# Rotary positions moved into the projection stream, a later wait for the router weights, and an earlier clearing of the expert accumulator

## The reference, cut to what matters

```
h   = layer_norm(x) * (1 + scale) + shift
p   = h @ w_in                          # q, k, v of A and B, conv inputs, q, k, v, o, gates of D
yA  = windowed attention of rope(qA), rope(kA), vA    # 8 heads, 2 key heads, latent rows are rotated
yB  = neighbourhood attention of qB, kB, vB
yC  = silu(layer_norm(depthwise conv over 31 tokens of a * sigmoid(gate)))
yD  = mLSTM, forwards and backwards
z   = sum_i sigmoid(h @ w_gate_i + b_gate_i) * (y_i @ w_branch_i)
x   = layer_norm(2**0.5 * x + g1 * (z @ w_out))
h2  = layer_norm(x) * (1 + scale2) + shift2
aff = softmax(h2 @ w_router)            # 16 experts; each takes its best tokens (64 latent, 32 context)
m   = sum_e put back(aff_e * (silu(xg @ w1_e) * (xg @ w3_e)) @ w2_e)
x   = layer_norm(2**0.5 * x + g2 * m)
```

## Time and profile before

| | us |
|---|---|
| three runs: median (lowest, highest) | 4023.34 (4022.8, 4026.16) |
| the profiled execution: its time | 4029.46 |
| its span, first to last instruction | 4027.8 |
| PE busy | 3587.6 (89%) |
| PEld busy | 2743.3 (68%) |
| DVE busy | 2335.1 (58%) |
| ACT busy | 1588.6 (39%) |
| POOL busy | 741.7 (18%) |
| mean granted TensorE clock | 0.944 of full speed |

### The profile page before, as it was taken

The page is one execution under the profiler, slowest core; times in us unless marked ns, Lnnn a source line. Parts: engine busy times, 40 slices in busy tenths (PEclk is TensorE's granted clock), DMA queues, the critical chain, the costliest instruction groups (busy, mean ns, idle before and its releaser), DMA issues. The chain is left out here.

```text
span 4027.8 us, 49164 instructions
## 1 busy us (share of the span) xinstructions
PE 3587.6 (89%) x18834; PEld 2743.3 (68%) x18834; DVE 2335.1 (58%) x3474; ACT 1588.6 (39%) x2055; POOL 741.7 (18%) x403
## 2 busy tenths in 40 slices
PE   8797889899998869999998699798899868999994
PEld 3697569888887756666664388578766655666663
DVE  2295761511111659999897464751322258999996
ACT  0321762511110236666662222553311126666662
POOL 0100012111110013332231100011222103233221
PEclk9899999899999889999998799899999979999997
DMA  9121022011112228888887621131122217999994
GB/s 317 61 73 69 21 79 71 12 68 56 40 63 74 94 82 306 311 309 311 308 307 273 206 79 63 43 100 53 37 94 94 84 64 270 327 325 334 331 324 152
DMA packets 329455, 632.73 MB, mean 157 GB/s; under 512 B 12288, under 2 KB 102480, under 8 KB 322880
## 3 DMA queue, kind: packets, MB, share of 16 engines
q1 hardware_dynamic: 309056, 557.88, 40.0%
q0 software_dynamic: 20240, 72.64, 5.3%
HBM read 613.95 MB, written 16.52 MB: 157 GB/s over the span
## 5 line engine op out<-in xcount | busy, mean ns | idle before, releaser
L733 PE MATMUL ps<-hx,part 128*128 128x384 f32 (+2 forms) x4704 | 928.9, 357 | 32.2 <-DVEq L474 17.3
L733 PEld LDWEIGHTS ps<-hx,part 128*128 128x128 f32 x4704 | 834.4, 190 | 115.7 <-DVEq L474 18.5
L1094 PE MATMUL ps<-part,hx 128*96 128x512 f32 x3072 | 759.0, 397 | 38.3 <-DVE part L1868 31.1
L1094 PEld LDWEIGHTS ps<-part,hx 128*96 128x96 f32 x3072 | 492.7, 163 | 249.1 <-DVE part L1868 49.7
L1868 DVE TENSOR_TENSOR part<-raw,part 128x2048 fp32r<-128x2048 f32 x256 | 615.4, 2404 | 26.1 <-ACT part L1356 24.3
L1356 ACT ACTIVATE part<-raw 128x2048 fp32r<-128x2048 f32 x256 | 489.9, 1914 | 214.0 <-PE ps L1094 188.9
L460 POOL TENSOR_TENSOR part<-raw,part 128x2048 fp32r<-128x2048 f32 x52 | 237.6, 4570 | 1165.9 <-ACT part L457 1165.9
L1094 PE MATMUL ps<-hx 128*96 128x512 f32 x1536 | 378.9, 395 | 4.0 <-DVE hx L1868 2.4
L1094 PEld LDWEIGHTS ps<-hx 128*96 128x96 f32 x1536 | 247.3, 162 | 112.9 <-POOL hx L680 5.7
L733 PE MATMUL ps<-part,hx 128*128 128x256 f32 (+2 forms) x2208 | 307.5, 301 | 15.5 <-DVEq L474 15.5
L733 PEld LDWEIGHTS ps<-part,hx 128*128 128x128 f32 x2208 | 289.0, 194 | 30.9 <-DVEq L474 16.2
(11 more groups left out here) (244 smaller groups left out, 3807.8 us busy)
## 6 DMA issues: line engine op xcount, KB each, us to landing
raw<-in_w_exp_gate SPq DMA_DIRECT2D x128, 1024.0 KB, 5.3
raw<-in_w_exp_up SPq DMA_DIRECT2D x128, 1024.0 KB, 5.3
raw<-in_w_exp_down SPq DMA_DIRECT2D x128, 1024.0 KB, 5.4
raw<-in_w_mod SPq DMA_DIRECT2D x48, 1024.0 KB, 6.4
raw<-in_w_in SPq DMA_DIRECT2D x44, 1024.0 KB, 4.8
raw<-in_w_gate SPq DMA_DIRECT2D x32, 1024.0 KB, 5.4
area<-in_bias POOLq DMA_DIRECT2D x32, 512.0 KB, 4.0
raw<-in_w_branch SPq DMA_DIRECT2D x16, 1024.0 KB, 8.6
```

The source lines that it names most:

```text
L733: last = mm(dst, a, b, start=i == 0, stop=i == len(pairs) - 1)
L1094: last = mm(ps[0:CAP, bank, :], x, y, start=kh == 0 and a == 0, stop=kh == 1 and a == len(pairs) - 1)
```

## The change

- **Rotary in the stream.** The rotary stage is gone. TensorE does its six matmuls between groups of `project`: blocks 0 and 1 ahead of groups 12 and 13, blocks 2 and 3 ahead of 16 and 17, blocks 4 and 5 ahead of 26 and 27 (`ROPE_AT`), in PSUM banks 6 and 7, so `depth` goes from 4 to 3. From the third on, each waits for DVE's first instruction of the rotary block two before it. DVE does its three instructions for each: two blocks after the rest of w_in block S_AB+6, two after that of S_AB+8, and two at the end, after `conv_tapped` and the rest of the last block of the stage. The taps are spread over seven shares, not eight (31 and 14 taps). The scratch `rope_s` has one buffer, not two, in the place of the sigmoid's scratch.
- **POOL.** It stores `yc_d` as soon as the taps are through, ahead of its two rests, and waits for the store's landing before it leaves the stage.
- **Router weights.** TensorE waits for `router_in` ahead of the first logits (t = 2).
- **Accumulator.** POOL clears `acc` at the start of the router stage, ahead of its wait for `slots`. DVE makes the first two rests of the experts before it clears `put`, `y_hi` and `y_lo`, and TensorE no longer waits for `put_zero`.

```
@@ -72,6 +72,9 @@
+ROPE_AT = (12, 13, 16, 17, 26, 27)
+
+
@@ -315,9 +318,9 @@
         kB = y_v[3]
         vB, _ = cut(ys, 2 * FB * TOK, NT, BW)
         cpad, oc = cut(work, o, FB, LSEG + CSEG)
-        rope_s, _ = cut(work, o, 2, LAT)
         yc, oc = cut(work, oc, FB, TOK)
         csg, oc = cut(work, oc, TOK)
+        rope_s = csg[:, 0:LAT]
         rope_t, oc = cut(work, oc, 2, LAT)
         rot, oc = cut(work, oc, P)
         bias, oc = cut(work, o, 4, LAT)
@@ -587,11 +590,9 @@
                 load(rot, A["rope"][:, 2 * LAT:2 * LAT + P]).then_inc(*S("rope_in", l).by(16))
                 pool.wait_ge(*S("rope_in", l).at(32))
                 pool.wait_ge(*S("conv_tapped", l).at(1))
+                load(yc_d[:, :, 0:full * P], yc[:, :, 0:full * P]).then_inc(*S("yc_out", l).by(16))
                 split.mixers_from(l, S_D)
                 split.mixers_to(l, S_D + 2)
-                load(yc_d[:, :, 0:full * P], yc[:, :, 0:full * P]).then_inc(*S("yc_out", l).by(16))
-                st.leave()
-
                 pool.wait_ge(*S("yc_out", l).at(16))
                 st.leave()
 
@@ -645,6 +646,7 @@
                 pool.wait_ge(*S("x1_out", l).at(16 * full))
                 st.leave()
 
+                nc.gpsimd.memset(acc, 0.0).then_inc(*S("acc_zero", l).by(1))
                 pool.wait_ge(*S("slots", l).at(1))
                 for v, row in enumerate((slotR, affR)):
                     load(slot_d[l, v, :, 0:full * P], row[0:E, 0:full * P]).then_inc(*S("slots_out", l).by(16))
@@ -653,7 +655,6 @@
 
                 st.leave()
 
-                nc.gpsimd.memset(acc, 0.0).then_inc(*S("acc_zero", l).by(1))
                 r0 = l * LAYER_BLOCKS + B_EXP
                 h0 = l * (MIX_SPLITS + EXP_BLOCKS * E) + MIX_SPLITS
                 with turns(pool, E // 2) as i:
@@ -804,15 +805,18 @@
                         last.then_inc(*pa.by(B_IN + b, j))
 
 
-                project("ab_part", AB_GROUPS, S("ab_out", l), 4,
-                        {0: lambda: pe.wait_ge(*S("conv_glu", l).at(3)), 2: lambda: pe.wait_ge(*S("conv_glu", l).at(4))})
-                st.leave()
-
-                for j in range(6):
+                def rope(j):
+                    if j == 0:
+                        pe.wait_ge(*S("rope_in", l).at(32))
+                        pe.wait_ge(*S("ab_out", l).at(6))
                     if j >= 2:
                         pe.wait_ge(*S("rope_done", l).at(j - 1))
                     src = y_v[0][:, j, 0:LAT] if j < FB else kA[:, j - FB, 0:LAT]
-                    mm(ps[:, j % 2, :], rot, src, start=True, stop=True).then_inc(*S("rope_rot", l).by(1))
+                    mm(ps[:, 6 + j % 2, :], rot, src, start=True, stop=True).then_inc(*S("rope_rot", l).by(1))
+
+                project("ab_part", AB_GROUPS, S("ab_out", l), 3,
+                        {0: lambda: pe.wait_ge(*S("conv_glu", l).at(3)), 2: lambda: pe.wait_ge(*S("conv_glu", l).at(4)),
+                         **{ROPE_AT[j]: lambda j=j: rope(j) for j in range(6)}})
                 st.leave()
 
                 us, gs = head_pairs(l), turn_groups(l)
@@ -1005,7 +1009,6 @@
 
                 op = out_parts(l)
                 ws = [take() for _ in range(4)]
-                pe.wait_ge(*S("router_in", l).at(16))
                 for t in range(full + 2):
                     if t < full:
                         if t >= 2:
@@ -1024,6 +1027,8 @@
                         last.then_inc(*S("xn_T", l).by(1))
                     if t >= 2:
                         pe.wait_ge(*S("h2_tmp", l).at(t - 1))
+                        if t == 2:
+                            pe.wait_ge(*S("router_in", l).at(16))
                         passes(ps[:, 6, (t - 2) * E:(t - 1) * E], [(h2t[:, t % 2, k, :], wr[:, k, :]) for k in range(KD)]
                                ).then_inc(*S("r_logits", l).by(1))
                 st.leave()
@@ -1054,7 +1059,6 @@
                 ncomb = 2 * full
                 n += EXP_BLOCKS * E
                 pe.drain().then_inc(*S("e_comb", l).by(1))
-                pe.wait_ge(*S("put_zero", l).at(1))
 
                 def scatter(c, before):
 
@@ -1196,9 +1200,7 @@
                             split.mixers_to(l, b + 3)
 
 
-                copies("ab_part", AB_GROUPS, S("ab_out", l), 4)
-                st.leave()
-
+                copies("ab_part", AB_GROUPS, S("ab_out", l), 3)
                 st.leave()
 
                 us, gs = head_pairs(l), turn_groups(l)
@@ -1502,24 +1504,32 @@
                 glu(3)
                 convolve(4)
                 split.mixers_to(l, S_AB + 2)
-                share = -(-len(taps) // (S_D - S_AB - 2))
-                for q in range(S_AB + 2, S_D):
-                    convolve(share)
-                    split.mixers_to(l, q + 1)
-                own.wait()
-                dve.drain().then_inc(*S("conv_tapped", l).by(1))
-                st.leave()
-
-
-                dve.wait_ge(*S("rope_in", l).at(32))
-                for j in range(6):
+                def rope(j):
+
                     q = y_v[0][:, j, 0:LAT] if j < FB else kA[:, j - FB, 0:LAT]
                     dve.wait_ge(*S("rope_rot", l).at(j + 1))
-                    V.tensor_tensor(rope_s[:, j % 2, :], ps[:, j % 2, :], rope_t[:, 1, :], ALU.mult).then_inc(*S("rope_done", l).by(1))
+                    own.wait()
+                    V.tensor_tensor(rope_s, ps[:, 6 + j % 2, :], rope_t[:, 1, :], ALU.mult).then_inc(*S("rope_done", l).by(1))
                     own(V.tensor_tensor(q, q, rope_t[:, 0, :], ALU.mult))
                     own.wait()
                     dve.wait_ge(*S("rope_done", l).at(j + 1))
-                    V.tensor_tensor(q, q, rope_s[:, j % 2, :], ALU.add)
+                    own(V.tensor_tensor(q, q, rope_s, ALU.add))
+
+                share = -(-len(taps) // (S_D - S_AB - 3))
+                for q in range(S_AB + 2, S_D - 1):
+                    convolve(share)
+                    split.mixers_to(l, q + 1)
+                    if q == S_AB + 6:
+                        dve.wait_ge(*S("rope_in", l).at(32))
+                    if q in (S_AB + 6, S_AB + 8):
+                        rope(q - S_AB - 6)
+                        rope(q - S_AB - 5)
+                assert not taps
+                own.wait()
+                dve.drain().then_inc(*S("conv_tapped", l).by(1))
+                split.mixers_to(l, S_D)
+                rope(4)
+                rope(5)
                 st.leave()
 
                 us, gs, withbias = head_pairs(l), turn_groups(l), biased(l)
@@ -1915,6 +1925,9 @@
                                                    ).then_inc(*S("e_yL", l).by(1))
 
 
+                for s in range(AHEAD):
+                    if not rest_rank(s)[0]:
+                        rest(0, s)
                 for v, cols in ((put, TOK), (y_hi, D), (y_lo, D)):
                     own(V.tensor_scalar(v[0:CAP, :], consts[0:CAP, 0:1].to_broadcast([CAP, cols]), 0.0, None, ALU.mult))
                 own.wait()
@@ -1924,9 +1937,6 @@
                 dve.drain().then_inc(*S("e_put", l).by(1))
                 dve.drain().then_inc(*S("e_acc", l).by(1))
                 dve.drain().then_inc(*S("e_yL", l).by(2))
-                for s in range(AHEAD):
-                    if not rest_rank(s)[0]:
-                        rest(0, s)
                 with turns(dve, E // 2 - 1) as i:
                     turn(i, False)
                 turn(E // 2 - 1, True)
```

23 lines of the change are left out of this document (11 added, 12 removed).

## The result

| | before | after |
|---|---|---|
| median of 4 runs each (lowest, highest), us | 4023.75 (4022.8, 4026.16) | 3961.73 (3957.57, 3967.02) |
| ratio after to before, 95% interval | | 0.9846 (0.9829, 0.9863) |
| the profiled execution, us | 4029.46 | 3967.02 |
| its span, us; mean granted clock | 4027.8; 0.944 | 3965.4; 0.950 |

The change takes 62.0 us, or 1.5%. The prediction was 3965.7.

What follows compares the result with a forecast made beforehand. PE, busy 89% of the span, was taken as the bound, with its idle stretches at stage borders to remove. 10.2 + 17.4 + 18.0 + 12.0 = 57.6 us off 4029.5, adjusted to the median, gave 3965.7 us; range 3951 to 3985.

Steps and rivals of the forecast that it cites:

- The chosen case: Whole kernel: every term as worked out, within its bounds, giving 3965.7 us, own range 3953 to 3978; chance 0.70.
- Layer 0's rotary work: Layer 0, projections to attention: rotary stage and store wait go, PE gains 5.4 us of matmuls and 8.1 of waits; 10.2 less.
- its last rival: Layer 0's projections: PE's new waits bring its clock to 1.2 GHz and it stays there, 4066 us; chance 0.03.
- the third wait: Layer 0's projections: PE waits 1.6 us for DVE's rest after the last share of 30 taps.
- the slower rival: The same as its last rival: PE's clock stays low in layer 0's projections, 4066 us; chance 0.03.
- Layer 1's rotary work: Layer 1, projections to attention: PE adds 5.4 us alone, without waits for DVE; attention starts 17.4 us earlier, bounds 14 and 18.
- What ended the stage: Projections to attention, before: the landing of POOL's convolution store, 9.9 us after its issue in layer 0, released PE.
- Router weights: Output projection: PE starts when the last w_out block lands, 10.2 us earlier in layer 0, 7.8 in layer 1; 18.0 less.
- the upper bound: Output projection: 23 us less if PE starts with the clock still up, saving some of 3.4 us in either layer.
- Experts: Start of the experts: PE's first scatter 6.0 us earlier in each layer, 12.0 less in all, bounds 7 and 13.
- the case that gives 9.2: Start of the experts: DVE's first rest waits 1.4 us for POOL's to end, so the part brings 9.2, not 12.0.
- Memset in the router: Router stage: POOL's memset beside DVE's small instructions costs 0; at worst 5.2 us in each layer, 10.4 together.

Runs made afterwards that it cites:

- e12: The changed kernel run once more, nothing altered: 3963.41 us, ratio to before 0.9853.
- e4: The changed kernel with later rotary matmuls, all DVE rotary work behind the taps, and eight tap shares again: 3954.95 us, ratio to before 0.9836.
- e8: The kernel before with three pairs of PSUM banks, not four, in the projections of A and B: 4024.57 us, ratio to before 1.0001.
- e1: The changed kernel with only the rotary part and the earlier store kept, the other two parts undone: 3993.79 us, ratio to before 0.9923.
- e5: The changed kernel with the convolution result's store behind POOL's two rests, its landing still waited for: 3984.83 us, ratio to before 0.9906.
- e2: The kernel before with only the later wait for the router weights: 4005.20 us, ratio to before 0.9955.
- e11: The changed kernel with e4's late rotary work and a separate wait for each w_out block when first needed: 3943.46 us, ratio to before 0.9801.
- e3: The kernel before with only the earlier memset and the new order at the experts' start: 4010.75 us, ratio to before 0.9968.
- e7: The changed kernel with DVE's clearing ahead of its first two rests again, memset still in the router: 3968.93 us, ratio to before 0.9860.
- e6: The changed kernel with POOL's memset back at the start of the experts: 3970.27 us, ratio to before 0.9871.

## Why the prediction was right

The chosen case, as worked out, is the one that came: 3965.7 predicted, 3961.73 measured. Step by step:

**Layer 0's rotary work: 10.2 predicted, 10.2 in the trace** (11.5 of lead less the 1.3 that the span had at its start). The sum was right; two of its parts were not, and that they cancel is luck. From the start of the block with 144 short matmuls to the end of the projections PE takes 117.4 us before (256.90 to 374.26), 130.6 in after (255.59 to 386.18), 129.2 in e12 (255.25 to 384.49) and 122.5 in e4 (254.83 to 377.28). So the six matmuls alone cost 5.1 (e4), for the 5.4 predicted, and what DVE's lateness adds is 8.1 in after and 6.8 in e12, for 8.1. But PE's idle times in after are 1.43, 3.27 and none, 4.7 in all and not 8.1. The first is short mainly because DVE's five shares with their rests took 92.8 us (214.89 to 307.65) and not 94.0. The third is gone because PE's own pace fell in between, which the prediction had left to its last rival. Windows of after and of e12_after_again, the same program:

```profile
326.00:330.00 4.00, 0.97 (x6) 0.65 (x4) 4.00 (x5) 2.61 (x2) 0.00 (x0) 0.93 0.00 0
330.00:336.00 6.00, 5.75 (x18) 5.75 (x19) 6.00 (x12) 0.00 (x0) 0.00 (x0) 0.50 0.49 175
336.00:342.00 6.00, 6.00 (x36) 6.00 (x35) 6.00 (x13) 0.36 (x1) 0.00 (x0) 0.97 0.01 3
```

```profile
330.00:336.00 6.00, 6.00 (x35) 6.00 (x36) 6.00 (x12) 0.00 (x0) 0.00 (x0) 1.00 0.50 178
```

And e12's PE behind the wait:

```profile
329.87 16.91 PE L734 MATMUL ps<-hx,part 128*128 128x384 f32 x96 [3.24 <-DVE part L463]
347.96 17.54 PE L734 MATMUL ps<-part,hx 128*128 128x256 f32 x144 [1.17 <-DVE part L463]
```

In after the clock went to 1.2 GHz at the wait of 3.27 us and was back some 6 us later; the same 96 matmuls took 19.68 us where e12 has 16.91. That hid the third wait, which e12 shows with 1.17. So waits and clock are 4.7 + 2.8 = 7.5 us in the one profile and 1.41 + 3.24 + 1.17 = 5.8 in the other; the 0.6 and 1.0 left up to 8.1 and 6.8 are small losses around the waits that I did not trace. e4 removed them all: they were what the early rotary work cost. This is the mechanism of the slower rival, seen at 2.8 us; the long fall in the clock that it needed did not come. The Trainium skill (TensorE: Matmul & The Clock Gate, on a second failure mode) describes a clock that cycles where PSUM banks are turned with brief pauses; with depth 3 alone PE did not pause and the clock stayed at 1.00 (e8), so no run here shows that form.

**Layer 1's rotary work: 17.4 predicted, 18.2 in the trace** (the lead goes from 27.8 to 46.0). PE waited for nothing (window of after):

```profile
2360.00:2487.00 127.00, 127.00 (x826) 120.29 (x825) 80.30 (x103) 28.13 (x42) 5.74 (x2) 1.00 0.23 84
```

From the start of the block with the 144 short matmuls (x144, 128x144) to the end of the projections it is 105.9 us before (2404.94 to 2510.82) and 111.1 after (2376.34 to 2487.43): 5.2 for the six matmuls, for 5.4. To the attention it is 135.6 us before (2540.57) and 118.3 after (2494.59), so this stage gives 17.4, as predicted, and the 0.8 above it is from unchanged code. The two layers give 28.4 in the trace and e1 30.5 by itself, for 27.6.

**What ended the stage** was POOL's store landing, as read from the earlier trace rows. e5 puts the store last and gets the old idle time back, 16.94 us and about 23 us of time.

**Router weights: 18.0 predicted, 19.1 by e2.** In the trace the lead grows by 11.7 and 7.2. The starts are as predicted, 4.84 and 4.99 us after the last issue. In layer 0 the first tile took 15.9 us (1264.53 to 1280.40) where 17.1 was taken, which is what the upper bound had named: the clock was at 0.72 over the tile's first 6 us, where it was 0.50 before (1283 to 1289). In layer 1 the tile took 17.1 and the clock was 0.50 over its first 6 us (3132 to 3138), after 5.02 us of idle time and not 4.87, so a short wait alone does not bring it back. DVE never waited for a row vector. e11 shows that the rest of this was to be had too.

**Experts: 12.0 predicted, 14.3 in the trace** (20.6 to 27.7 and 53.9 to 61.0), 13.5 by e3. The term was mis-sized by one step: the clearing with its drains was to hold the first scatter until 10.7 us after ACT's start, and `e_yL` was up at about the end of block 0, 9.56 and 9.88 us after it. The clearing is 1.75 us and not 3.6. The first matmul came 5.2 us after ACT's start where 4.4 was taken: DVE's two rests took 5.00 and 5.34 us, against 4.49 where POOL only issues loads (e7) or runs the memset (e6). So it was DVE that was held up, and not POOL, whose rest of the tokens took 1.81 us; the prediction had taken it the other way. In both layers DVE's first rest, begun beside POOL's, ended 2.14 us behind the end of POOL's (1455.95 behind 1453.81, 3277.96 behind 3275.82), and one rest alone takes 2.29. The Trainium skill (SBUF — State Buffer, the part on the two sides of its ports) says that a DVE instruction with two SBUF inputs and a GpSimd one that reads SBUF exclude each other for a whole instruction, and the trace agrees to within 0.15 us: it looks as if DVE's rest got under way only when POOL's was over. By their durations that cost the rests 0.5 and 0.9 us and not the 1.4 of the case that gives 9.2, and POOL was through 3.0 us after ACT's start and not 3.4.

**Memset in the router: 0 predicted, 0 in the trace.** From the router's first maximum to its last pick it takes 33.49 us before and after. e6 prices the old place at 4.7 and 3.8 us at the starts.

**The sum.** By the trace 10.2 + 18.2 + 18.9 + 14.3 = 61.6, against 57.6. (The low end of the prediction's range was put at a gain of 38 us; its terms give 37.0.) The lead at the last add is 62.4; the 0.8 between is what unchanged code gave and took, from +1.5 to -3.1 us a stage.

## What to carry to other kernels

Read what ends each idle stretch at a stage border: a stage that waits for all engines also waits for the last thing the slowest of them issued, and a store that no one needs yet can be that. When work is moved into a full stage, follow the engine with the least slack block by block and put the new work behind its last deadline; here this brought the next stage 8.1 us forward. A wait for several loads at once, ahead of work that needs only the first, costs the time of all the others.

## What the runs showed that was not expected

- The same code in the mLSTM stage of layer 0 took 77.84 us in after, 75.74 before and 73.53 in e4, at other granted clocks. Windows of its last part, after and then e4:

```profile
767.00:784.80 17.80, 13.90 (x92) 13.45 (x91) 6.93 (x25) 3.97 (x10) 2.53 (x2) 0.81 0.00 0
```

```profile
757.00:770.50 13.50, 9.60 (x81) 9.25 (x80) 5.57 (x20) 3.97 (x10) 1.26 (x1) 1.00 0.00 0
```

  So some 4 us of a difference between two single profiles can be the clock's alone. The runs of after spread over 9.5 us; those of before spread over 3.4 in the first set of 4, and over 12.3 in the set of 16 beside e1.
- A wait of 3.27 us was followed by 1.2 GHz in one execution and one of 3.24 us in the same place by 2.4 GHz in another. Six profiles have this wait, of 3.24 to 3.27 us: the 96 matmuls behind it took 19.5 to 19.7 us in four (after, e1, e5, e7) and 16.9 in two (e6, e12).
- DVE's clearing of 96 partitions took 1.75 us alone and 4.00 us beside POOL's cast and rest of the tokens (e7). Beside the memset one of its three instructions alone took 5.65 us. The memset itself took 5.22 us wherever it stood.
